# GpSimd's order in the expert stage: a main tile's addition to the output is issued in the next expert's turn, behind the gather of that expert's first lot

## The reference

```
y = (silu(xt[tok] @ w1[e]) * (xt[tok] @ w3[e])) @ w2[e] * gate
out[tok] += y            # x + g2 * moe: the rows of out already hold the residual
```

## Time and profile before

| | |
|---|---|
| median of 3 runs | 2413.15 us (2411.49 to 2414.89) |
| the profiled execution's own time | 2409.21 us |
| its span | 2407.5 us |
| granted clock of PE, mean | 0.97 |
| PE busy | 2227.6 us (93%) |
| DVE busy | 1430.2 us (59%) |
| ACT busy | 1181.7 us (49%) |
| POOL busy | 500.8 us (21%) |
| expert stage | from about 1600 us to the end |
| rows gathered, line 2752 | 53 DMAs |
| main additions, line 2770 | 32 DMAs |
| lot additions, line 2761 | 20 DMAs |

### The profile page before, as it was taken

One profiled execution on the slowest core, in us unless ns is written; L12 is line 12 of the kernel. 1 busy time (PEld: TensorE's weight loads), 2 busy tenths in 40 slices (PEclk: granted clock), 3 DMA queues, 4 the chain that ended last, 5 costly groups with the idle time before them and its releaser, 6 DMA issues. The chain is left out here.

```text
span 2407.5 us, 43378 instructions
## 1 busy us (share of the span) xinstructions
PE 2227.6 (93%) x15189; PEld 1549.2 (64%) x15190; DVE 1430.2 (59%) x2488; ACT 1181.7 (49%) x2106; POOL 500.8 (21%) x772
## 2 busy tenths in 40 slices
PE   5998999999979999789999999968899999999998
PEld 2335777888856666456666666746666776666775
DVE  4456686232325555555555555466677887666886
ACT  4556322222134444355555555345566666555674
POOL 2662111000001101001222222341222122222122
PEclk8999999999989999899999999979999999999999
DMA  8895222122374543522222221359897988887994
GB/s 303 279 272 139 62 53 79 56 85 62 78 207 98 124 100 89 171 54 80 73 74 71 62 80 58 130 181 330 299 317 254 371 308 290 287 257 252 325 330 145
DMA packets 242118, 414.31 MB, mean 172 GB/s; under 512 B 25601, under 2 KB 129365, under 8 KB 236915
## 3 DMA queue, kind: packets, MB, share of 16 engines
q1 hardware_dynamic: 198048, 354.24, 44.6%
q0 software_dynamic: 18800, 44.94, 7.6%
q10 hardware_dynamic: 25125, 13.18, 2.0%
HBM read 344.83 MB, written 76.85 MB: 175 GB/s over the span
## 5 line engine op out<-in xcount | busy, mean ns | idle before, releaser
L937 PE MATMUL ps_proj<-sb_hTh,sb_winh 128*128 128x512 f32 x576 | 234.4, 407 | 5.2 <-DVE sb_hTl L1089 2.5
L938 PE MATMUL ps_proj<-sb_hTl,sb_winh 128*128 128x512 f32 x576 | 226.5, 393 | 0.0
L939 PE MATMUL ps_proj<-sb_hTh,sb_winl 128*128 128x512 f32 x576 | 224.9, 390 | 0.0
L2258 DVE CUSTOM_DVE_ANT_0 sb_lead<-ps_S,sb_mask 128x640 f32<-128x640 f32 x124 | 102.0, 823 | 87.8 <-PE ps_S L1987 82.0
L2141 ACT ACTIVATE sb_lead<-sb_lead,sb_nm 128x640 f32<-128x640 f32 x128 | 106.3, 830 | 79.2 <-DVE sb_nm L2262 77.6
L1062 ACT COPY sb_rope_or_conv<-ps_proj 128x512 f32<-128x512 f32 x48 | 28.2, 588 | 222.0 <-PE ps_proj L939 147.7
L937 PEld LDWEIGHTS ps_proj<-sb_hTh,sb_winh 128*128 128x128 f32 x576 | 108.8, 189 | 34.6 <-issue 4.1
L2135 ACT COPY sb_lead<-ps_PT 128x512 f32<-128x512 f32 x160 | 89.4, 580 | 74.3 <-PE ps_PT L1979 74.3
L938 PEld LDWEIGHTS ps_proj<-sb_hTl,sb_winh 128*128 128x128 f32 x576 | 108.7, 189 | 25.9 <-issue 4.1
L939 PEld LDWEIGHTS ps_proj<-sb_hTh,sb_winl 128*128 128x128 f32 x576 | 108.5, 188 | 24.2
L2770 POOL DMA_INDIRECT out<-sb_by,sb_rows_out x32 | 69.7, 2177 | 254.1 <-issue 240.1
(11 more groups left out here) (355 smaller groups left out, 5530.0 us busy)
## 6 DMA issues: line engine op xcount, KB each, us to landing
sb_lead<-in_exp_w SPq DMA_DIRECT2D x32, 2048.0 KB, 14.6
sb_w<-in_exp_w SPq DMA_DIRECT2D x32, 2048.0 KB, 9.1
sb_raw<-in_exp_w SPq DMA_DIRECT2D x32, 2048.0 KB, 14.7
sb_ada<-in_ada_w SPq DMA_DIRECT2D x16, 1536.0 KB, 7.7
scr_filt<-sb_fout SPq DMA_DIRECT2D x128, 128.0 KB, 3.1
sb_yh<-scr_filt SPq DMA_DIRECT2D x64, 256.0 KB, 4.9
scr_hy_in<-sb_hcT ACTq DMA_DIRECT2D x12, 1024.0 KB, 5.5
sb_win<-in_w_in SPq DMA_DIRECT2D x9, 1024.0 KB, 6.0
```

What stands on the lines that cost most here:

```text
L937: pe.matmul(mp[:, r % 4, 0:N], a, high[:, k, :], start=(k == 0), stop=False)
L938: pe.matmul(mp[:, r % 4, 0:N], a, low[:, k, :], start=False, stop=False)
L939: ins = pe.matmul(mp[:, r % 4, 0:N], b, high[:, k, :], start=False, stop=(k == KT - 1))
L2258: ve.tensor_tensor_reduce(out=pr[:, p, :], in0=mixer_scores if nx.n == 0 and p % 2 else scores_of[p % 2], in1=mask[:, edge, mask_of[p % 2] ...
```

## The change

Only POOL's program in the expert stage changes. Before, the order in an expert was: for each lot gather and lot addition; then gather; then the main addition, at the main tile's end. After it, a main tile's addition is no longer written at the end of its expert but in the next expert: if that expert has lots, behind the gather that its first lot allows; if it has none, first of all. The last expert's main addition is written behind the loop. The waits of each instruction are the same as before.

```diff
-            def lot(n, x, ex, par, half, before):
-                gather(n + 2)
+            def add_lot(n, x, ex, before):
                 pool.wait_ge(y_ok, n + 2)
                 pool.wait_ge(scat_m, 16 * ex + 16)
                 pool.wait_ge(scat_l, 16 * before + 16)
...
-            def main(n, ex, par, half, last, lots):
-                gather(n + 2)
+            def add_main(n, ex, lots):
                 pool.wait_ge(y_ok, n + 2)
                 pool.wait_ge(scat_m, 16 * ex + 16)
                 pool.wait_ge(scat_l, 16 * lots + 16)
...
+            def first():
+                many, _ = span(pool, 0)
+                gather(2)
+                with pool.If(many > 1):
+                    gather(3)
+                add_main(0, 0, 0)
+                with pool.If(many > 1):
+                    add_lot(1, 0, 0, 0)
+                with pool.If(many > 2):
+                    with pool.Fori(1, many - 1) as b:
+                        gather(b + 3)
+                        add_lot(b + 1, b, 0, 0)
+
+            def one(ex, behind_main=True):
+                many, lots = span(pool, ex)
+                n = lots + ex
+                with pool.If(many > 1):
+                    gather(n + 2)
+                if behind_main:
+                    add_main(n - 1, ex - 1, lots)
+                with pool.If(many > 1):
+                    add_lot(n, lots, ex, lots)
+                with pool.If(many > 2):
+                    with pool.Fori(1, many - 1) as b:
+                        gather(n + b + 2)
+                        add_lot(n + b, lots + b, ex, lots)
+                gather(n + many + 1)
...
-            total = experts(pool, lot, main)
+            first()
+            one(1, False)
+            with pool.Fori(1, NE // 2 - 1) as pair:
+                one(2 * pair)
+                one(2 * pair + 1)
+            one(NE - 2)
+            one(NE - 1)
+            total = pool.value_load(info[0:1, 2, NE - 1:NE], min_val=0, max_val=TILES - NE) + NE
+            add_main(total - 1, NE - 1, total - NE)
```

## The result

The changed kernel is slower: 2425.1 us median (2418.67 to 2433.77, 17 runs) against 2413.99 us (2406.44 to 2419.87, 17 runs); ratio 1.0047, 95% interval 1.0035 to 1.0059, so +11.3 us by the ratio (8 to 14). The forecast was 2437, +24 us.

A forecast was written before the change was run, and what follows sets the result against it. PE was taken as the bound, busy 763 of 805 us, with an equally long chain of additions through DVE. 21.5 + 1.6 (clock) + 1 (one-lot experts) = +24 us on 2409.2, 2433; forecast median 2437, 8-in-10 range 2416 to 2448.

The forecast's parts named there:

- rival 2: Intervals from main to first lot addition shrink in part, to their lower ends: +7 us, 2420; chance 15%.
- the late chain's own shift: Main addition, first lot's addition, DVE's second-lot output: main addition issued 4.95 us later, the rest moving with it.
- the five experts: Experts with several lots, at 1721, 1814, 2066, 2139, 2176: +2.4, +4.6, +5.0, +4.9, +4.6, together 21.5 us.
- the clock: PE's new waits of some 5 us in four main tiles bring slow clock: 0.4 us each, +1.6, bounds 0 and 6.4.
- the experts with one lot: Next gather stands behind the later lot addition, 0.4 us late at 1760; 1 us for all, bounds 0 and 8.
- The second chain is as long as PE's: Main addition, first lot's addition, DVE's second-lot output, low weights: already as long as PE's; idle 0.33 us or none.
- the four experts named: Main tiles of experts at 1721, 1814, 2139, 2176: PE stands some 5 us for the low part of w3.
- I keep these intervals.: From main to first lot addition: 8.54 us at 1814, 9.13, 9.89, 10.38 elsewhere, taken unchanged; bounds 7.3 and 13.4.
- rival 1: Interval from main to lot addition falls by the same 5 us; gain of 14.8 us stays: 2398; chance 6%.
- 0.9 us until the next indirect DMA: On POOL, between the gather's issue and the moved main addition: 0.9 us, bounds 0 and twice that.
- The expert with three lots: At 2066: gather behind the late lot addition, rows +3.4 us late, slow product +1.6; together +5.0, bounds +2.6 and +7.4.
- The scale: +24 us added to the profiled execution's 2409.2 gives 2433; the median, 4 us above that execution, gives 2437.

The follow-up runs named there:

- before_two_outputs: Kernel before, with two buffers for a lot's output and its row numbers instead of one; ratio to before 1.0001 (0.9988 to 1.0015).
- lots_behind_too: Changed kernel with two buffers for a lot's output, and inside an expert each lot's addition issued one gather later; ratio to before 0.9988 (0.9972 to 1.0005).
- two_outputs: Changed kernel, with two buffers for a lot's output and its row numbers instead of one; ratio to before 1.0047 (1.0029 to 1.0066).

## Why the prediction was wrong, step by step

The direction, the place and the mechanism held; the size didn't: 24 us forecast, 11 measured, nearer to rival 2 (+7) than to the forecast. The measured 2425.1 lies inside the stated range of 2416 to 2448, near its lower end. The term that failed is the late chain's own shift: the intervals from main to lot addition, which were kept as they had been. Of the error of 12.8 us (24.1 for 11.3), 5.7 lie in the five experts (21.5 and 1.6 for the clock, against 17.4), 1.0 in the experts with one lot, and 6.1 between the two traces and the medians.

- *The second chain is as long as PE's.* Right. `before_two_outputs` removes it and gains nothing; the new order makes it longer, and four new waits of PE appear in the four experts named.
- *"I keep these intervals."* This is the step that failed. From main to lot addition the interval shrank in all five experts: 9.89 to 9.15, 8.54 to 7.61, 10.38 to 8.30, 9.13 to 7.47, 9.49 to 7.77, together 7.1 us. In four of the five each of the three traces with the moved addition lies below each of the three without; at 1721 they touch (9.15 to 9.62 against 9.63 to 9.89). From the lot's addition to DVE's output it took 7.01 us at 1814 (from 7.96), 7.08 at 2139 (from 8.26) and 7.16 at 2176 (from 7.72), but 8.77 at 1721, where I had put 7.96.
- *Why the chain got shorter* is open; the traces narrow it down. The gather doesn't leave the rings: while the main addition at 1814 was landing, GpSimd's queue moved 0.93 MB before and 1.05 MB after. What fell is what the weights' queue moved in that time (packets, MB, share; before from 1814.48 to 1822.00, after from 1822.81 to 1829.50):

```profile
q1 hardware_dynamic: 391, 1.54, 50.3%
...
q1 hardware_dynamic: 123, 0.25, 11.7%
```

  It fell in the same way at 2139 (1.54 to 0.20 MB) and 2176 (1.49 to 0.20), and by about half at 1721 and 2066 (2.41 to 1.28, 2.62 to 1.12). So the moved addition meets less of the weights' loading. That this is why it lands sooner is my reading, and no run varied it by itself. The prediction says of the weights, for rival 1, that they are "not yet loading at that moment in some experts"; something of the kind held for part of the way.
- *0.9 us until the next indirect DMA.* Measured 0.30 in four of the five experts, 0.6 us less of shift in each, and 0.88 at 2176. The 0.85 that it came from stands between a copy and a gather that reads what the copy wrote.
- *The clock.* 0.4 us each was forecast. Beyond the 7.39 us from line 2631 to line 2646 it took 0.9 us more at 1721, nothing at 1814, 1.1 at 2139 and 1.9 at 2176: 3.9 us for 1.6. The granted clock behind PE's wait was 0.55 at 1721 (1746.60 to 1749.96), 1.00 at 1814, 0.65 at 2139 (2172.00 to 2175.00) and 0.50 at 2176.
- *The sum redone.* With the measured pieces the forecast's own sum comes out in the experts with two lots. At 2139: 4.95 - 0.60 (issue) - 1.66 (interval) - 1.18 (lot's landing) + 1.1 (clock) = 2.6, measured 2.6. At 1814: 4.95 - 0.60 - 0.93 - 0.95 - 0.33 = 2.1 for 1.9. At 2176: 4.95 - 0.02 - 1.72 - 0.56 - 0.30 + 1.9 = 4.3 for 4.3.
- *The expert with three lots.* +5.0 forecast, +5.9 measured, and that is luck. The gather was issued 2.9 us sooner than forecast (2087.55 less the offset of 5.87 there, for 2084.6), and landed in 8.0 us where I had put 4.6.
- *Experts with one lot.* Forecast 1 us, measured 0 in the changed kernel. The danger was real, as the 5.3 us of `lots_behind_too` show.
- *The scale.* The terms were differences to one execution and were added to a median. The profiled execution of before lay 4.8 us under its median (2409.21 for 2413.99), that of after 2.9 over (2427.99 for 2425.1), so the two traces stand 7.7 us further apart than the medians, which is where the 6.1 us between 17.4 and 11.3 come from. A part may be the longer wait for weights ahead of the turn at 1721, absent in the first trace of before and in the three traces of the moved addition. Another may be that old waits at the gathers come and go and a chain added beside them covers them; no run tells how much.
- *What I didn't see.* The next gather behind the first lot's addition I counted only in the expert with three lots. It is held in the experts with two lots too, under the cover of DVE's wait; `two_outputs` laid it bare, with the slow copy on top.

## What to carry to other kernels

When an instruction in an in-order queue is moved back, list everything that waits for it and everything written behind it, and price each as if the others were gone: here two holds covered each other, and taking away one gave nothing. Keep an interval that contains a DMA's landing as a range, since moving the DMA changes what is moved beside it: here the weights' 1.54 MB fell to 0.25. Before a sum is made on one trace, ask for a second: here two traces of one kernel differ by 8.6 us in the stretch in question.

## What the runs showed of the hardware

GpSimd's copy of 128 row numbers takes 0.18 us in most of its 53 instances and up to 1.0 us in a few, but in `two_outputs` it took 2.9 to 3.7 us in the four experts with two lots. In the one at 2139 (us of before) it ended at 2175.81, and VectorE's row of three subtractions, each of two SBUF operands, at 2172.29 + 3.49 = 2175.78:

```profile
2172.14 3.67 POOL L2755 COPY sb_rows_in<-sb_brec 128x1 int32 x1
```

```profile
2172.29 3.49 DVE L2610 TENSOR_TENSOR sb_w3l<-sb_raw,sb_w3h 128x1024 fp32r<-128x1024 f32 x3
```

The Trainium skill, "SBUF — State Buffer", section "SBUF: two separate sides", says that VectorE and GpSimd share a pair of ports as an exclusive lock, which a VectorE instruction with two SBUF inputs takes against a GpSimd instruction that reads SBUF. These two rows agree, and go further: the copy stood through all three VectorE instructions and not just the one that was running. The other three copies in `two_outputs` end 0.02 to 0.04 us behind such a row as well, and in `after` one stood through six of VectorE's instructions in a row, the last of them ending at 2019.90 + 3.49 = 2023.39:

```profile
2017.78 5.65 POOL L2749 COPY sb_rows_in<-sb_brec 128x1 int32 x1
```

At 1814 and at 2139 the copy's own row begins 0.15 us ahead of the subtractions, and it waited all the same. The issue of a gather shows the same. The six of 6.35 to 6.74 us, the one of 6.50 above among them, all end 0.94 to 0.96 us behind the end of such a row of VectorE (1786.34 + 3.49 = 1789.83 for the end at 1790.78), and a gather's issue takes 1.05 us by itself. That the lock is the cause was not tried by a run of its own. In the expert at 2139 of `two_outputs` the gather went out 10.1 us after the turn began, where it was 2.6 before; 3.5 us of these 7.5 are the copy's.
